# Attention in a decoder layer: ScalarE casts a turned tile ahead of the next tile's exponentials

## The chip, the core and the metric

One core of a Trainium2 chip runs the whole program. The metric is the time of one execution on the device in microseconds (us), as the median of several runs. The engines are PE (TensorE, matmuls and transposes), ACT (ScalarE), DVE (VectorE), POOL (GpSimd), and SP, whose queue issues most of the DMAs. Each engine works through its own instructions in a fixed order and waits for the others by semaphores.

## The reference

One layer (`DEPTH = 1`) of 1024 tokens with 1024 values each: forgetting attention with 16 heads of 64 values, a layer norm, then a mixture of 64 experts (8 per token) with one shared expert, and a second layer norm. The change touches attention alone:

```
for qb in range(S // Q):                       # Q = 128 queries
    t0, t1 = qb * Q, (qb + 1) * Q
    logits = einsum('bqhd,bkhd->bhqk', q[:, t0:t1], k[:, :t1]) * scale
    logits = logits + c[:, :, t0:t1, None] - c[:, :, None, :t1]
    p = softmax(where(causal, logits, -inf), axis=-1)
    outs.append(einsum('bhqk,bkhd->bqhd', p, v[:, :t1]))
```

`c` is a running sum of log gates. The softmax runs over the keys up to each query.

## The kernel before

Attention handles one head after another. Within a head it walks over eight query tiles of 128 queries, `t` = 0 to 7. Tile `t` has (t + 1) x 128 scores per query. They are cut into slots of at most 512 columns: tiles 0 to 3 have one slot each, tiles 4 to 7 have two, which makes 12 slots (0 to 11) a head. For every tile the work goes round three engines:

- PE computes the scores of a slot (lines 817 to 820) into one of three PSUM banks (`slot_banks`: two `bank`, one half of `out_ps`). The bank of slot n is free once the exponential of slot n - 3 has run.
- DVE takes the maximum of each slot (`maxima`, L1548) and, for two slots, the smaller of the two negated maxima (L1552). The result is `nm`.
- ACT takes the exponentials (`exponentials`, L1193) into `probs` (four buffers) and sums them.
- PE turns the slot, block by block, by transposes (`turns`, L847) into one of two banks of `k_ps` (`key_banks`).
- ACT casts the turned slot to its high half `pt_hi` (`turned_high`, L1204). DVE subtracts this to get the low half `pt_lo` (`turned_low`, L1559). The turned bank is free after that; turn number u waits for the low half of turn u - 2.
- PE multiplies high and low halves with the values (`weigh_v`, L868), once for tiles 0 to 3 of a head and once for tiles 4 to 7.

The order on each engine is written out by hand in a function `head` of its own. The turns lag by one tile: in step t PE computes the scores of tile t, some chunks of the next head's query and key projection (`project`, L80 to L82), and then turns the slots of tile t - 1. In step 0 the turned slots 10 and 11 are those of the head before, in step 2 PE also does `weigh_v` for the second half of the head before, and in step 5 for the first half of this head.

Other pieces sit between: `weights_hi`/`weights_lo` (L1165, L1500) split the next heads' projection weights; `take` moves a projected half from `q_ps` to SBUF (ACT L1184 and L1185, DVE L1539 and L1541); `low_values` (ACT L1212) and `normalise` (DVE L1574 and L1578) finish a half of a head's output. Turns 2 and 5 are not slots but the reciprocal sums (`rec`, L853). Turn 7 waits for `normalise` of the second half, as its bank holds those sums.

DVE's order within a step is: maxima of tile t, then `take` or `normalise` or weights where the step has them, then the low halves. In step 2 this reads: maximum of tile 2, `take` of the next head, low half of turn 4. In step 3: maximum of tile 3, `normalise`, low half of turn 6.

Of the kernel before, what the change touches and what calls it, by code (L numbers as in the profile page):

```python
# [5 lines left out]
P = 128  # L6
BANK = 512
ALU = mybir.AluOpType
# [4 lines left out]
AX_X = mybir.AxisListType.X  # L13
# [3 lines left out]
TT = T // P  # L17
# [67 lines left out]
def build(nc, x, w_in, b_f, w_out, ln1_g, ln1_b, router, router_bias, w_gate, w_up, w_down, ws_gate, ws_up,  # L85
          ws_down, ln2_g, ln2_b, out):
    with ExitStack() as ctx:
# [3 lines left out]
        def sb(n, s, d=F32, c=ctx):  # L91
            return c.enter_context(nc.sbuf_tensor(n, s, d))
# [27 lines left out]
        with ExitStack() as early:  # L120
# [3 lines left out]
            with ExitStack() as x1s:  # L124
                xt_hi = sb("xt_hi", [P, DC, T], F32R, c=x1s)
                xt_lo = sb("xt_lo", [P, DC, T], F32R, c=x1s)
                wqk = sb("wqk", [P, DC, P], c=x1s)
                wqk_hi = sb("wqk_hi", [P, DC, P], F32R, c=x1s)
                wqk_lo = sb("wqk_lo", [P, DC, P], F32R, c=x1s)
                with ExitStack() as a:  # L130
                    wv = sb("wv", [P, 2, DC, VC], c=a)
                    wv_hi = sb("wv_hi", [P, 2, DC, VC], F32R, c=a)
                    wv_lo = sb("wv_lo", [P, 2, DC, VC], F32R, c=a)
                    v_out = sb("v_out", [P, 2, 2 * VC // DH, 2, DH], F32R, c=a)
                    wf = sb("wf", [P, DC, HEADS], c=a)
                    wf_hi = sb("wf_hi", [P, DC, HEADS], F32R, c=a)
                    wf_lo = sb("wf_lo", [P, DC, HEADS], F32R, c=a)
                    bf = sb("bf", [P, HEADS], c=a)
                    zt = sb("zt", [HEADS, T], c=a)
                    z = sb("z", [P, TT, HEADS], c=a)  # L140
                    zabs = sb("zabs", [P, TT, HEADS], c=a)
                    zexp = sb("zexp", [P, TT, HEADS], c=a)
                    zlog = sb("zlog", [P, TT, HEADS], c=a)
                    zmin = sb("zmin", [P, TT, HEADS], c=a)
                    gate8 = sb("gate8", [P, TT, HEADS], c=a)
                    upto = sb("upto", [P, T], c=a)
                    c_hi = sb("c_hi", [HEADS, T], F32R, c=a)
                    c_lo = sb("c_lo", [HEADS, T], F32R, c=a)
                with ExitStack() as b:
                    qk = [[sb(f"{n}{i}", [P, T], F32R, c=b) for n in ("q_both", "q_ones", "k_twice", "k_rest")] for i in range(2)]  # L150
                    va = [sb(f"va{i}", [P, TT, P], F32R, c=b) for i in range(2)]
                    probs = [sb(f"probs{i}", [P, BANK], c=b) for i in range(4)]
                    pt_hi = sb("pt_hi", [P, TURNED, P], F32R, c=b)
                    pt_lo = sb("pt_lo", [P, TURNED, P], F32R, c=b)
                    heads_sum = sb("heads_sum", [DH, BANK], c=b)
                    nm = sb("nm", [P, TT], c=b)
                    nm2 = sb("nm2", [P, 2], c=b)
                    ssum = [sb(f"ssum{i}", [P, 2, TT], c=b) for i in range(2)]
                    rsum = sb("rsum", [P, TT // 2], c=b)
                    rec = [sb(f"rec{i}", [P, TT], c=b) for i in range(2)]  # L160
# [101 lines left out]
        S = {}  # L262
# [873 lines left out]
        def _(act):  # L1136
# [22 lines left out]
            def weights_hi(h, piece):  # L1159

                act.wait_ge(wqk_in[piece], 32 * h + 32)
                if not (static(h) and h == 0):
                    act.wait_ge(S["proj"], 3 * h + (piece - 1))
                c = slice(piece * DC // 2, (piece + 1) * DC // 2)
                a.copy(wqk_hi[:, c], wqk[:, c]).then_inc(S["wqk_hi_ok"], 1)  # L1165
# [15 lines left out]
            def take(h, par, half):  # L1181
                act.wait_ge(S["proj"], 3 * h + (2 * half + 1))
                r = slice(half * BANK, (half + 1) * BANK)
                a.mul(qk[par][0][0:DH, r], q_ps[0:DH, r], SCALE)  # L1184
                a.copy(qk[par][2][0:DH, r], q_ps[DH:P, r]).then_inc(S["ev_hi"], 1)  # L1185

            def exponentials(h, par, t):
                act.wait_ge(S["maxed"], TT * h + (t + 1))
                for k, n in enumerate(OF_TILE[t]):
                    w = SLOTS[n][2]  # L1190
                    if not (static(h) and NS * h + n < 4):
                        act.wait_ge(S["turned_ps"], NS * h + (n - 3))
                    a.activation(probs[n % 4][:, 0:w], slot_banks[n % 3][:, 0:w], ACT.Exp, bias=nm[:, t:t + 1],  # L1193
                                 accum_out=ssum[par][:, k, t:t + 1]).then_inc(S["exped"], 1)

            def turned_high(h, u):

                _, back, n = TURNS[u]
                act.wait_ge(S["turned_ps"], NS * h + (NS * back + n + 1))
                half = 0 if n < HALF_SLOTS[0] else 1  # L1200
                if not (static(h) and h + back < 1):
                    act.wait_ge(S["pv"], 2 * h + (2 * back + half - 1))
                b, step, count = turned_blocks(n)
                a.copy(pt_hi[:, b:b + (count - 1) * step + 1:step, :],  # L1204
                       key_banks[u % 2][:, 0:count * P].rearrange("p (j q) -> p j q", q=P)).then_inc(S["turned_hi"], 1)

            def low_values(h, half):

                act.wait_ge(S["pv"], 2 * h + (half + 1))
                if not (static(h) and 2 * h + half == 0):  # L1210
                    act.wait_ge(S["normed"], 2 * h + half)
                a.copy(heads_sum[:], pv_ps[DH:P, :]).then_inc(S["low_ok"], 1)  # L1212
# [6 lines left out]
            def head(p, par, first=False, left=HEADS):  # L1219
                h = 2 * p + par  # L1220
                for t in range(TT):
                    exponentials(h, par, t)
                    if t == 0 and not first:
                        if left > 1:
                            weights_hi(h + 1, 1)
                        turned_high(h, 0)
                        turned_high(h, 1)
                        take(h, par, 1)
                    elif t == 1:
                        turned_high(h, 3)  # L1230
                    elif t == 2:
                        if left > 1:
                            take(h + 1, 1 - par, 0)
                        turned_high(h, 4)
                    elif t == 3:
                        if not first:
                            low_values(h - 1, 1)
                        turned_high(h, 6)
                    elif t == 4:
                        turned_high(h, 7)  # L1240
                    elif t >= 5:
                        if t == 6 and left > 2:
                            weights_hi(h + 2, 0)
                        if t == 7:
                            low_values(h, 0)
                        for u in (2 * t - 2, 2 * t - 1):
                            turned_high(h, u)
                    if left == 1 and t >= 2:
                        split_wo(range(t - 2, t - 1))

# [233 lines left out]
        def _(dve):  # L1484
# [50 lines left out]
            def take(h, par, half):  # L1535
                q_both, _, k_twice, k_rest = qk[par]
                dve.wait_ge(S["ev_hi"], 2 * h + (half + 1))
                r = slice(half * BANK, (half + 1) * BANK)
                dve.scalar_tensor_tensor(out=q_both[DH:P, r], in0=q_ps[0:DH, r], scalar=SCALE, in1=q_both[0:DH, r], op0=ALU.mult,  # L1539
                                         op1=ALU.subtract)  # L1540
                dve.tensor_tensor(k_rest[0:DH, r], q_ps[DH:P, r], k_twice[0:DH, r], ALU.subtract).then_inc(S["ev_lo"], 1)  # L1541

            def maxima(h, t):

                for k, n in enumerate(OF_TILE[t]):
                    dve.wait_ge(S["score"], NS * h + (n + 1))
                    one = len(OF_TILE[t]) == 1
                    dve.tensor_reduce(nm[:, t:t + 1] if one else nm2[:, k:k + 1], slot_banks[n % 3][:, 0:SLOTS[n][2]], AX_X, ALU.max,  # L1548
                                      negate=True).then_inc(S["maxed"] if one else S["max_step"], 1)
                if not one:  # L1550
                    dve.wait_ge(S["max_step"], TT * h + 2 * (t - 3))
                    dve.tensor_tensor(nm[:, t:t + 1], nm2[:, 0:1], nm2[:, 1:2], ALU.min).then_inc(S["maxed"], 1)  # L1552

            def turned_low(h, u):
                _, back, n = TURNS[u]
# [432 lines left out]
```

## Time and profile before

| | us |
|---|---|
| median of 3 runs | 1902.46 |
| lowest and highest run | 1892.62, 1911.94 |
| the profiled execution, time | 1887.1 |
| its span in the trace | 1885.4 |
| PE busy | 1650.2 (88%) |
| DVE busy | 1200.7 (64%) |
| ACT busy | 1017.2 (54%) |
| stretch with attention, from the trace | about 155 to 690 of the span |
| one pair of heads within it | 64.8 to 64.9 |

The page's shares are means over the whole program. The experts (after 690 us) have other limits than attention. What an edit of attention is worth must be read inside the stretch of one head, where the timeline gives, for each engine, the start and length of each instruction and what ended the idle time before it.

### The profile page before, as it was taken

To read this page: it belongs to the slowest core of one execution; us is meant where nothing else is said; L and a number is where in the kernel's file an instruction comes from. 1 tells how busy PE (TensorE), PEld (TensorE's weight loads), DVE (VectorE), ACT (ScalarE), POOL (GpSimd) and SP (SyncE) were. 2 spreads that over 40 slices of the span, in tenths; PEclk is the share of its full clock that TensorE was granted. 3 is DMA by queue.
4 is the path that set the end of the run, shared out by engine and by line. 5 is a ranking of instruction groups with operands and counts; after the bars stand their busy time and mean duration, and the time that the engine had idled before them with its cause. 6 is when DMAs were issued, how large, how long until landed. Compare 5 with 4: busy or idle time off the path is not lost.

```text
span 1885.4 us, 31807 instructions
## 1 busy us (share of the span) xinstructions
PE 1650.2 (88%) x8302; PEld 1323.5 (70%) x8303; DVE 1200.7 (64%) x2030; ACT 1017.2 (54%) x1672; POOL 474.1 (25%) x486
## 2 busy tenths in 40 slices
PE   7995888888888859989999999999999999999960
PEld 5894666666676648777877777777777777787740
DVE  3212656556565556885566777777776777787836
ACT  3113545554555443333566676766766676777732
POOL 0000000000000000545144444444344443544420
PEclk9998999999999869889999999999999999999995
DMA  5313222212121214264799999998999899999956
GB/s 178 114 68 76 51 51 47 53 39 62 39 62 34 86 62 171 81 236 138 256 299 286 280 302 358 327 282 264 267 301 291 262 317 320 333 339 333 372 135 263
DMA packets 161508, 369.26 MB, mean 196 GB/s; under 512 B 53040, under 2 KB 73520, under 8 KB 161456
## 3 DMA queue, kind: packets, MB, share of 16 engines
q1 hardware_dynamic: 136272, 284.21, 44.2%
q0 software_dynamic: 25184, 84.39, 17.8%
q8 instruction: 28, 0.46, 0.1%
q14 instruction: 24, 0.20, 0.0%
HBM read 294.39 MB, written 65.77 MB: 191 GB/s over the span
## 4 chain that ended last, share of the span: by engine, by line
PE 46%; DVE 19%; issue 11%; DMA 11%; ACT 9%; POOL 2%; DVEq 1%; POOLq 1%; ACTq 1%; SPq 0%
DMA sums_scratch<-ys,sidx 5%; DVE nm L1548 5%; PE bank L969 4%; PE bank L975 4%; PE bank L972 4%; DVE pt_lo L1559 4%; PE out_ps L1027 3%; PE out_ps L1028 3%; DMA x_rows<-rows_scratch,gidx 3%; ACT probs L1193 3%; PE q_ps L959 3%; PE k_ps L1004 2%; PE k_ps L996 2%; PE k_ps L997 2%; PE bank L80 2%
## 5 line engine op out<-in xcount | busy, mean ns | idle before, releaser
L1778 DVE TENSOR_TENSOR gu_lo<-raw_gu,gu_hi 128x1024 fp32r<-128x1024 f32 x260 | 306.8, 1222 | 20.6 <-ACT gu_hi L1297 20.0
L1297 ACT CAST gu_hi<-raw_gu 128x1024 fp32r<-128x1024 f32 x260 | 252.7, 1048 | 0.0
L969 PE MATMUL bank<-gu_hi,xb_hi 128*128 128x512 f32 x576 | 235.0, 408 | 1.4 <-ACT ex L1289 1.3
L972 PE MATMUL bank<-gu_lo,xb_hi 128*128 128x512 f32 x576 | 227.6, 395 | 0.0
L1559 DVE TENSOR_TENSOR pt_lo<-k_ps,pt_hi 128x512 fp32r<-128x512 f32 (+1 forms) x192 | 100.9, 553 | 139.1 <-ACT pt_hi L1204 138.2
L1193 ACT ACTIVATE probs<-bank,nm 128x512 f32<-128x512 f32 (+3 forms) x128 | 73.9, 579 | 191.8 <-DVE nm L1552 107.6
L1778 DVE TENSOR_TENSOR dn_lo<-raw_dn,dn_hi 128x1024 fp32r<-128x1024 f32 x130 | 154.6, 1209 | 0.5 <-ACT dn_hi L1297 0.5
L641 POOL DMA_INDIRECT sums_scratch<-ys,sidx x64 | 114.2, 1784 | 131.4 <-DMA sums_scratch<-ys,sidx 76.8
L975 PE MATMUL bank<-gu_hi,xb_lo 128*128 128x512 f32 x576 | 146.2, 395 | 0.0
L576 POOL IOTA e<- 128x64 f32 x1 | 0.2, 190 | 550.6 <-DVE xs L1578 550.6
L1297 ACT CAST dn_hi<-raw_dn 128x1024 fp32r<-128x1024 f32 x130 | 129.5, 1046 | 0.0
L847 PE MATMUL k_ps<-ident,probs 128*128 128x128 f32 x576 | 94.5, 295 | 38.0 <-DVE pt_lo L1559 31.1
L969 PEld LDWEIGHTS bank<-gu_hi,xb_hi 128*128 128x128 f32 x576 | 109.5, 190 | 25.8 <-issue 2.5
L975 PEld LDWEIGHTS bank<-gu_hi,xb_lo 128*128 128x128 f32 x576 | 108.0, 187 | 26.4
L80 PE MATMUL q_ps<-xt_hi,wqk_hi 128*128 128x512 f32 x256 | 115.2, 450 | 11.9 <-DVE wqk_lo L1500 11.9
L972 PEld LDWEIGHTS bank<-gu_lo,xb_hi 128*128 128x128 f32 x576 | 108.9, 189 | 22.6
L996 PE MATMUL k_ps<-dn_hi,ht_hi 128*128 128x512 f32 x288 | 122.2, 424 | 1.4 <-ACT ht_hi L1326 1.4
L997 PE MATMUL k_ps<-dn_lo,ht_hi 128*128 128x512 f32 x288 | 117.6, 408 | 0.0
L847 PEld LDWEIGHTS k_ps<-ident,probs 128*128 128x128 f32 x576 | 70.9, 150 | 64.9 <-DVE pt_lo L1559 32.2
L959 PE MATMUL q_ps<-ident,x_rows 128*128 128x128 f32 x576 | 85.6, 295 | 29.8 <-DMA x_rows<-rows_scratch,gidx 24.1
L1318 ACT CAST xb_hi<-q_ps 128x1024 fp32r<-128x1024 f32 x72 | 73.1, 1016 | 67.3 <-PE q_ps L959 67.3
L1782 DVE TENSOR_TENSOR xb_lo<-q_ps,xb_hi 128x1024 fp32r<-128x1024 f32 x72 | 88.1, 1224 | 29.7 <-ACT xb_hi L1318 28.2
(268 smaller groups left out, 4123.8 us busy)
## 6 DMA issues: line engine op xcount, KB each, us to landing
raw_gu<-in_moe_w_gate_dram SPq DMA_DIRECT2D x128, 512.0 KB, 6.7
raw_gu<-in_moe_w_up_dram SPq DMA_DIRECT2D x128, 512.0 KB, 8.4
raw_dn<-in_moe_w_down_dram SPq DMA_DIRECT2D x128, 512.0 KB, 6.6
wqk<-in_fox_w_in_dram SPq DMA_DIRECT2D x66, 128.0 KB, 2.4
v_scratch<-v_out SPq DMA_DIRECT2D x32, 256.0 KB, 2.8
va<-v_scratch SPq DMA_DIRECT2D x16, 512.0 KB, 4.7
xs<-in_x_dram SPq DMA_DIRECT2D x8, 512.0 KB, 7.6
wv<-in_fox_w_in_dram SPq DMA_DIRECT2D x4, 1024.0 KB, 7.6
```

Of the source, the lines that this page charges most:

```text
L80: pe.matmul(out, w_hi, m_hi, start=start, stop=False, skip_group_check=True)
L847: i = pe.transpose(bank[:, j * P:(j + 1) * P], probs[n % 4][:, j * P:(j + 1) * P], ident[:])
L959: i = pe.transpose(ps[:, c * P:(c + 1) * P], v[:, c], ident[:])
L969: i = pe.matmul(o3, xb_hi[s][:, c], g_hi[:, :, c], start=c == 0, stop=False, skip_group_check=True)
L972: pe.matmul(o3, xb_hi[s][:, c], g_lo[:, :, c], start=False, stop=False, skip_group_check=True)
L975: i = pe.matmul(o3, xb_lo[s][:, c], g_hi[:, :, c], start=False, stop=c == DC - 1, skip_group_check=True)
L996: pe.matmul(k_ps[:, r], ht_hi[:, c], d_hi[:, c, r], start=c == 0, stop=False, skip_group_check=True)
L997: pe.matmul(k_ps[:, r], ht_hi[:, c], d_lo[:, c, r], start=False, stop=False, skip_group_check=True)
L1193: a.activation(probs[n % 4][:, 0:w], slot_banks[n % 3][:, 0:w], ACT.Exp, bias=nm[:, t:t + 1], accum_out=ssum[par][:, k, t:t + 1]).then_inc ...
L1297: a.copy(hi, raw).then_inc(S[done], 1)
L1559: dve.tensor_tensor(pt_lo[:, at, :], key_banks[u % 2][:, 0:count * P].rearrange("p (j q) -> p j q", q=P), pt_hi[:, at, :], ALU.subtract).t ...
L1778: dve.tensor_tensor(lo, raw, hi, ALU.subtract).then_inc(S[lo_ok], 1)
```

## The change

On ACT, each step of a head now begins with the casts of the slots that PE turns in that step, and the exponentials of the step's tile follow. Before, the exponentials came first and the casts were last in the step. The other pieces (`weights_hi`, `take`, `low_values` of the head before) keep their place behind the exponentials, and so now stand behind the casts too; `low_values` for the first half goes to the front of step 7. The two partial maxima of a tile get a place of their own for each tile (`nm2`). The orders of PE, DVE, POOL and SP stay as they were.

```diff
-                    nm2 = sb("nm2", [P, 2], c=b)
+                    nm2 = sb("nm2", [P, TT, 2], c=b)
...
                 for t in range(TT):
+                    if t == 7:
+                        low_values(h, 0)
+                    for u in ((0, 1), (3,), (4,), (6,), (7,), (8, 9), (10, 11), (12, 13))[t]:
+                        if not (first and TURNS[u][1]):
+                            turned_high(h, u)
                     exponentials(h, par, t)
                     if t == 0 and not first:
                         if left > 1:
                             weights_hi(h + 1, 1)
-                        turned_high(h, 0)
-                        turned_high(h, 1)
                         take(h, par, 1)
-                    elif t == 1:
-                        turned_high(h, 3)
-                    elif t == 2:
-                        if left > 1:
-                            take(h + 1, 1 - par, 0)
-                        turned_high(h, 4)
-                    elif t == 3:
-                        if not first:
-                            low_values(h - 1, 1)
-                        turned_high(h, 6)
-                    elif t == 4:
-                        turned_high(h, 7)
-                    elif t >= 5:
-                        if t == 6 and left > 2:
-                            weights_hi(h + 2, 0)
-                        if t == 7:
-                            low_values(h, 0)
-                        for u in (2 * t - 2, 2 * t - 1):
-                            turned_high(h, u)
+                    elif t == 2 and left > 1:
+                        take(h + 1, 1 - par, 0)
+                    elif t == 3 and not first:
+                        low_values(h - 1, 1)
+                    elif t == 6 and left > 2:
+                        weights_hi(h + 2, 0)
...
-                    dve.tensor_reduce(nm[:, t:t + 1] if one else nm2[:, k:k + 1], slot_banks[n % 3][:, 0:SLOTS[n][2]], AX_X, ALU.max,
+                    dve.tensor_reduce(nm[:, t:t + 1] if one else nm2[:, t, k:k + 1], slot_banks[n % 3][:, 0:SLOTS[n][2]], AX_X, ALU.max,
...
-                    dve.tensor_tensor(nm[:, t:t + 1], nm2[:, 0:1], nm2[:, 1:2], ALU.min).then_inc(S["maxed"], 1)
+                    dve.tensor_tensor(nm[:, t:t + 1], nm2[:, t, 0:1], nm2[:, t, 1:2], ALU.min).then_inc(S["maxed"], 1)
```

ACT's order in steps 2 to 4 of a middle head, before. L1193 is an exponential (128x384 is tile 2, the next 128x512 tile 3, then the two slots of tile 4), L1204 the cast of a turned slot (2x128 is turn 4, 3x128 turn 6, 4x128 turn 7), L1184 and L1185 the `take`, L1212 `low_values`:

```order
L1193 ACTIVATE probs,ssum<-out_ps,nm 128x384
L1184 ACTIVATE q_both<-q_ps 64x512
L1185 CAST k_twice<-q_ps 64x512
L1204 CAST pt_hi<-k_ps 128x2x128
L1193 ACTIVATE probs,ssum<-bank,nm 128x512
L1212 COPY heads_sum<-out_ps 64x512
L1204 CAST pt_hi<-k_ps 128x3x128
L1193 ACTIVATE probs,ssum<-bank,nm 128x512
L1193 ACTIVATE probs,ssum<-out_ps,nm 128x128
L1204 CAST pt_hi<-k_ps 128x4x128
```

And now, the same steps on ACT:

```order
L1204 CAST pt_hi<-k_ps 128x2x128
L1193 ACTIVATE probs,ssum<-out_ps,nm 128x384
L1184 ACTIVATE q_both<-q_ps 64x512
L1185 CAST k_twice<-q_ps 64x512
L1204 CAST pt_hi<-k_ps 128x3x128
L1193 ACTIVATE probs,ssum<-bank,nm 128x512
L1212 COPY heads_sum<-out_ps 64x512
L1204 CAST pt_hi<-k_ps 128x4x128
L1193 ACTIVATE probs,ssum<-bank,nm 128x512
L1193 ACTIVATE probs,ssum<-out_ps,nm 128x128
```

Each cast moved ahead of its step's exponential, of `take` in step 2 and of `low_values` in step 3.

ACT's order in steps 6 and 7 of a middle head, before. L1165 is `weights_hi`; the last two casts are turns 12 and 13, and the two 128x512 exponentials are slots 10 and 11:

```order
L1193 ACTIVATE probs,ssum<-out_ps,nm 128x512
L1193 ACTIVATE probs,ssum<-bank,nm 128x384
L1165 CAST wqk_hi<-wqk 128x512
L1204 CAST pt_hi<-k_ps 128x4x128
L1204 CAST pt_hi<-k_ps 128x2x128
L1193 ACTIVATE probs,ssum<-bank,nm 128x512
L1193 ACTIVATE probs,ssum<-out_ps,nm 128x512
L1212 COPY heads_sum<-out_ps 64x512
L1204 CAST pt_hi<-k_ps 128x4x128
L1204 CAST pt_hi<-k_ps 128x3x128
```

And now:

```order
L1204 CAST pt_hi<-k_ps 128x4x128
L1204 CAST pt_hi<-k_ps 128x2x128
L1193 ACTIVATE probs,ssum<-out_ps,nm 128x512
L1193 ACTIVATE probs,ssum<-bank,nm 128x384
L1165 CAST wqk_hi<-wqk 128x512
L1212 COPY heads_sum<-out_ps 64x512
L1204 CAST pt_hi<-k_ps 128x4x128
L1204 CAST pt_hi<-k_ps 128x3x128
L1193 ACTIVATE probs,ssum<-bank,nm 128x512
L1193 ACTIVATE probs,ssum<-out_ps,nm 128x512
```

Here two casts moved ahead of two exponentials, and `low_values` for the first half went with them.

## Rows read from the trace of the kernel before

**Rows 1.** The page's engines: busy us, share of the span, instructions.

```profile
PE 1650.2 (88%) x8302; PEld 1323.5 (70%) x8303; DVE 1200.7 (64%) x2030; ACT 1017.2 (54%) x1672; POOL 474.1 (25%) x486
```

**Rows 2.** PE in windows of two heads: length, busy, clock, DMA share, GB/s.

```profile
204.20:269.10 64.90, 56.05 (x298) 0.97 0.20 49
...
528.50:593.40 64.90, 56.17 (x298) 0.97 0.20 49
```

**Rows 3.** Who waited for whom, 204 to 630 us (12 to 13 heads): us, times, longest.

```profile
ACT probs L1193 <- DVE nm L1552: 114.0, 52, 2.7
DVE pt_lo L1559 <- ACT pt_hi L1204: 103.2, 52, 2.4
...
PE k_ps L847 <- DVE pt_lo L1559: 18.6, 24, 1.2
PE bank L817 <- ACT probs L1193: 14.6, 13, 1.2
PE q_ps L80 <- DVE wqk_lo L1500: 10.7, 13, 1.1
```

**Rows 4.** PE's timeline over one head: start, length, instruction, [idle before <- releaser].

```profile
412.67 0.50 PE L817 MATMUL out_ps<-k_twice,q_both 128*128 128x512 f32 x1 [0.66 <-ACT probs L1193]
...
414.95 0.99 PE L847 MATMUL k_ps<-ident,probs 128*128 128x128 f32 x7 [0.71 <-DVE pt_lo L1559]
416.34 0.32 PE L817 MATMUL bank<-k_twice,q_both 128*128 128x128 f32 x1 [0.40 <-issue]
...
417.32 0.50 PE L80 MATMUL q_ps<-xt_hi,wqk_hi 128*128 128x512 f32 x1 [0.48 <-DVE wqk_lo L1500]
...
420.17 1.09 PE L847 MATMUL k_ps<-ident,probs 128*128 128x128 f32 x8 [1.18 <-DVE pt_lo L1559]
...
421.80 0.28 PE L817 MATMUL bank<-k_twice,q_both 128*128 128x256 f32 x1
...
429.76 0.41 PE L847 MATMUL k_ps<-ident,probs 128*128 128x128 f32 x2
...
432.41 0.49 PE L847 MATMUL k_ps<-ident,probs 128*128 128x128 f32 x3
...
435.47 0.65 PE L847 MATMUL k_ps<-ident,probs 128*128 128x128 f32 x4 [0.42 <-DVE xs L1578]
...
437.79 0.39 PE L817 MATMUL bank<-k_twice,q_both 128*128 128x256 f32 x1 [1.19 <-ACT probs L1193]
```

**Rows 5.** ACT's timeline in steps 2 to 4 of the same head.

```profile
428.15 0.58 ACT L1193 ACTIVATE probs<-out_ps,nm 128x384 f32<-128x384 f32 x1 [1.43 <-DVE nm L1548]
...
430.20 0.37 ACT L1204 CAST pt_hi<-k_ps 128x256 fp32r<-128x256 f32 x1 [0.30 <-PE k_ps L847]
432.41 0.69 ACT L1193 ACTIVATE probs<-bank,nm 128x512 f32<-128x512 f32 x1 [1.84 <-DVE nm L1548]
...
433.21 0.58 ACT L1212 COPY heads_sum<-out_ps 64x512 f32<-64x512 f32 x1
433.82 0.48 ACT L1204 CAST pt_hi<-k_ps 128x384 fp32r<-128x384 f32 x1
```

**Rows 6.** DVE's timeline in the same steps.

```profile
429.93 0.68 DVE L1539 SCALAR_TENSOR_TENSOR q_both<-q_ps,q_both 64x512 fp32r<-64x512 f32 x1 [1.81 <-ACT k_twice L1185]
...
431.36 0.42 DVE L1559 TENSOR_TENSOR pt_lo<-k_ps,pt_hi 128x256 fp32r<-128x256 f32 x1
...
434.66 0.68 DVE L1578 TENSOR_TENSOR xs<-heads_sum,k_ps 64x512 f32 x1
435.37 0.56 DVE L1559 TENSOR_TENSOR pt_lo<-k_ps,pt_hi 128x384 fp32r<-128x384 f32 x1
435.85 0.68 DVE L1548 TENSOR_REDUCE nm<-bank 128x1 f32<-128x512 f32 x1
```

**Rows 7.** ACT's `low_values` in step 7 of three successive heads.

```profile
418.13 0.58 ACT L1212 COPY heads_sum<-out_ps 64x512 f32<-64x512 f32 x1
...
450.71 0.58 ACT L1212 COPY heads_sum<-out_ps 64x512 f32<-64x512 f32 x1
...
483.02 0.58 ACT L1212 COPY heads_sum<-out_ps 64x512 f32<-64x512 f32 x1
```

**Rows 8.** PE in two windows: length, busy, clock, DMA share, GB/s.

```profile
449.90:453.40 3.50, 3.31 (x9) 0.55 0.36 75
453.40:460.00 6.60, 6.60 (x38) 0.98 0.28 61
```

## The prediction

> **What bounds the kernel now.** I read the page's engines first: PE is busy 88% of the span, DVE 64%, ACT 54% [rows 1]. Attention alone, in windows of two heads, gives 64.9 us a pair with PE busy 56.1 of them; six windows in a row, of which the first and last are shown, differ by 0.1 us [rows 2]. So a head takes 32.4 us, PE works 28 of them (with its drains counted as work), and an edit to the order of ACT can win at most what PE waits. The waits [rows 3] show a circle. ACT's exponentials wait 114.0 us for the maxima, DVE's low halves wait 103.2 us for ACT's casts: in a step, DVE's maxima, ACT's exponentials, ACT's casts and DVE's low halves run one behind the other, although casts and low halves belong to the tile before and need nothing of this step's maxima. PE sees the end of that circle at three places a head: transposes behind a low half, 24 times and 18.6 us, scores behind an exponential, and the projection behind `wqk_lo`. The timeline of one head [rows 4] gives their size: idle 0.71, 0.40, 0.48 and 1.18 us from step 7 of a head to step 0 of the next, 0.42 before turn 7, and 1.19 and 0.66 before the second slot of tiles 5 and 7.
>
> **Part 1, what the new order wins: steps 7 and 0.** The casts of turns 12, 13, 0 and 1 no longer wait for the exponentials, so the low halves, the maxima behind them and `weights_lo` all run earlier. From the second slot's scores of tile 7 (412.67) to the scores of tile 1 (421.80) PE takes 9.13 us [rows 4]. The work in it, at the spacing at which unhindered matmuls of that head start (0.235 us for 512 columns, which is three to a projection chunk of 0.70; about 0.1 us a transpose), is 0.55 for the scores, four chunks 2.8, 15 transposes 1.5, tile 0's scores 0.3: 5.15 us. I leave 0.25 for a shorter wait on `wqk_lo`, whose DVE instruction still stands behind the maxima of tile 7. Gain: 9.13 - 5.4 = 3.7 us. The four idle pieces alone are 2.77, so the gain lies between 2.8 and 4.0.
>
> **Part 2, what it loses in step 0.** `weights_hi` for the second piece stands behind the two casts, and these behind PE's turns 0 and 1. After these turns: cast about 0.5, exponential 0.37, `weights_hi` 0.6, `weights_lo` 0.7, and four hand-overs of about 0.1: 2.6 us. PE has a chunk, tile 1's scores and another chunk to do, 1.7 us. Loss 0.9 us (before, the projection did not wait there at all); between 0.5 and 1.2.
>
> **Part 3, what it loses in steps 2 to 4.** In step 2 PE does 3.1 us of `weigh_v` before turn 4. The exponential of tile 2 and `take` ran under that (428.15 [rows 5]); now they stand behind the cast of turn 4 and cannot start before about 430.2. DVE's FIFO carries the delay on: its `take` is ahead of the low half of turn 4, for which turn 6 waits. From the cast at 430.20: cast 0.37, exponential 0.58, ACT's `take` until DVE begins 1.2, DVE's `take` 1.43 (429.93 to 431.36), low half 0.42 [rows 5, 6]; turn 6 starts at 434.25 in place of 432.41 [rows 4]. In step 3 the same again: turn 6 0.49, cast 0.48, exponential 0.80, `low_values` 0.62, DVE's sum 0.83 and product until PE starts 0.81; turn 7 starts at 438.3 in place of 435.47. In step 4 DVE's low half of turn 6 (0.48) and the two maxima (435.85 until ACT starts, 1.10) follow the product, then the exponential 0.84: the second slot of tile 5 comes at 440.7 in place of 437.79. Loss 2.9 us. The nearest bound from below is half of that, if DVE and ACT overlap more than I have them; from above 3.3. I take 2.8, as the hand-overs are counted twice in places.
>
> **Part 4, steps 5 to 7.** A second slot's scores (tiles 6 and 7) need the exponential of the first slot of the tile before, and this stands now behind two casts that wait for PE's own turns. For tile 7: last turn until the cast is done about 0.5, exponential 0.7, against the first slot's scores 0.5 that PE has meanwhile. The wait stays near 0.7 to 1.1 us, as it was (0.66). Turn 9 and `weigh_v` no longer wait for a low half, 0.2 us. Net 0.2 gained, between 0.5 gained and 0.5 lost. The two instructions for `nm2` only write to other addresses: nothing. The DMAs and SP's and POOL's queues keep their order; their waits (`copied`, `wqk_in`) are issued several us before they are needed, and I cost them at nothing.
>
> **Sum without the clock.** -3.7 + 0.9 + 2.8 - 0.2 = -0.2 us a head. The first head has no head before it, the last no projection; I count 15 heads: -3 us.
>
> **Part 5, the clock.** In the pairs of [rows 2] the mean granted clock is 0.97. It falls once a pair: from 449.9 on PE ran 9 matmuls in 3.5 us at a clock of 0.55 (the lower level, 1.2 GHz, for most of it), behind the idle pieces between steps 7 and 0; then it is back [rows 8]. There it costs little, since PE had another 1.18 us of idle behind it to eat into: the head with it took 32.58 us, the next 32.31 [rows 7]. The change moves the holes. They now stand before turn 6 (1.8), turn 7 (1.3) and the second slot of tile 5 (1.3), within some 7 us, and behind the last of them PE has 6 us of work with hardly a wait. A stretch of 3.4 us at half rate costs 1.7 there less what little slack there is, 1.4 us, if it falls there. How often is not to be had from these rows. Bounds: never (0) and in every head (1.7 us a head). I take two heads in five, near the one in two of now, since the new holes are larger but those between steps 7 and 0 close: 1.4 x 0.4 = 0.56 us a head. What the clock costs now, 32.58 - 32.31 = 0.27 a pair or 0.14 a head [rows 7], goes off: 0.4 us a head, 6 us in all. The Trainium skill (TensorE: Matmul & The Clock Gate, "What's actually happening") says that the ramp's penalty is under 1% of a typical span and not to be fitted; by that the clock's term would be left out and the time would be 1899. The rows' 1% is the very bound that decides here, so I keep it.
>
> **The number.** -3 + 6 = +3 us. The profiled execution took 1887.1 us, so its like would take 1890; it stood 15 us (0.8%) below the median, all of which I put to the spread of runs (1892.62 to 1911.94). Against the median: 1902.5 + 3 = 1905.5, rounded to 1906.
>
> **The rivals.** "Within 1%" (19 us) is about what a measurement of this kernel can tell from no change.
>
> A, the forecast: gains in steps 7 and 0 and losses in steps 2 to 4 cancel; 1906, its own range 1893 to 1918. For it: the two chains are read from the same head, row by row. Chance 0.64.
>
> B, slower: the clock drops in every head. The place is the stretch behind the second slot of tile 5; the price 1.7 us x 15 = 25 us, with part 1 to 4's -3 and the present clock loss given back (-2): 1923. It decides if the idle before turns 6 and 7 and that slot (4.4 us of 8) lowers the clock each time. For it: now the clock falls behind idle pieces that together are 2.8 us of 8, but only in every second head; so the point is near. Against: the pair of holes varies by head. The Trainium skill has this as a rule (same page, "HAM oscillation — how this bites in real kernels"): a loop that waits too long in each turn starts each turn at the lower clock. By that rule it is this rival's time. With losses at their upper bounds B reaches 1930. Chance 0.19.
>
> C, faster: DVE and ACT take up the delay of step 2, as in part 3's lower bound or better. Only the gains of parts 1 and 4 and part 2's loss stay: (-3.7 + 0.9 - 0.2) x 15 = -45 us, 1857; with half of part 3, -3 + 6 - 21 = -18 us, 1884. It decides if `take` did not have to wait for the cast; against it stands the written order, which leaves ACT nothing else to do. Chance 0.10.
>
> D, the order does not matter: the casts in their new place end no earlier because PE's turns are late anyway. ACT's cast at 430.20 waited for PE by 0.30 [rows 5], which speaks for it in step 2; the 103.2 us speak against it elsewhere. 1902. Chance 0.07.
>
> **Range and chances.** The range takes A's and most of B's, and the near end of C: 1887 to 1926. Slower by over 1% (above 1921.5): most of B and a little of A, 0.17. Faster by over 1% (below 1883.4): C, 0.10. Same: 0.73.
>
> **What would show it.** In the profile after: PE's idle before the transposes and the first projection chunk between steps 7 and 0 gone or under 0.3 us (part 1); a wait for `wqk_lo` of about 0.9 between tile 1's first and second projection chunk (part 2); transposes x3 idle 1.8 behind `pt_lo` and transposes x4 idle over 1 behind `xs` (part 3); DVE's low halves waiting far less than 103.2 us, ACT's casts waiting for PE tens of us instead; a pair of heads of 64.5 to 66 us; low clock after the scores of tile 5 and not between heads (part 5). The prediction is wrong if the waits in steps 2 and 3 are under half of what I have, or if a pair takes over 67 us.

## The result: 1.2% slower

| | before | changed |
|---|---|---|
| median of 11 runs, us | 1894.56 | 1920.06 |
| lowest to highest | 1886.65 to 1911.94 | 1912.74 to 1922.92 |
| profiled execution, time / span | 1887.1 / 1885.4 | 1913.6 / 1911.9 |

The ratio to before is 1.0116, with a 95% interval of 1.0088 to 1.0144. That is also the ratio of the means of the 11 runs, 1918.4 and 1896.4 us, so the change costs 22 us; the two medians alone would give 1.0135.

The first thing to see in the profile after is what did not change. The page's engine line (busy us, share of the span, instructions), to be read against [rows 1], has the same instruction counts, and busy times within 1%:

```profile
PE 1657.4 (87%) x8302; PEld 1331.0 (70%) x8303; DVE 1204.1 (63%) x2030; ACT 1016.5 (53%) x1672; POOL 472.5 (25%) x486
```

So no work was added; the 26.5 us of span are waiting and clock. PE in windows of two heads (length, busy, clock, DMA share, GB/s), against 64.9 us and a clock of 0.97 in every pair before [rows 2]:

```profile
223.90:289.70 65.80, 54.69 (x300) 1.00 0.21 49
289.70:358.60 68.90, 57.78 (x299) 0.95 0.19 46
358.60:428.70 70.10, 58.99 (x299) 0.93 0.19 45
428.70:497.10 68.40, 57.30 (x298) 0.95 0.19 46
497.10:562.80 65.70, 54.60 (x298) 1.00 0.20 48
```

Two pairs are at full clock, and take 65.7 to 65.8 us: this is the price of the new waits alone, 0.4 us a head. The other three hold the lower clock in part and take 2.7 to 4.4 us more. The mean of the five is 67.8 us, over the 67 at which the prediction calls itself wrong. The waits of PE in 204 to 630 us (us in total, times, longest), the answer to [rows 3]:

```profile
PE k_ps L847 <- DVE pt_lo L1549: 21.4, 13, 1.7
PE k_ps L847 <- DVE xs L1568: 16.9, 13, 1.3
PE bank L817 <- ACT probs L1193: 14.8, 13, 1.2
PE out_ps L817 <- ACT probs L1193: 12.3, 13, 0.9
PE q_ps L80 <- DVE wqk_lo L1490: 6.1, 12, 0.5
```

Transposes waited 24 times for a low half before, twice a head and up to 1.2 us; now once a head and 1.7 us. The wait for `xs` (the product of `normalise`) is new in this size; before, it was 2.7 us in 6 waits. The waits behind ACT and DVE turned over:

```profile
ACT pt_hi L1204 <- PE k_ps L847: 213.5, 100, 3.8
DVE q_both L1529 <- ACT k_twice L1185: 54.4, 13, 4.4
DVE pt_lo L1549 <- ACT pt_hi L1204: 47.6, 38, 2.2
DVE wqk_lo L1490 <- ACT wqk_hi L1165: 31.7, 12, 2.6
```

DVE's low halves wait 47.6 us for ACT's casts where it was 103.2, as the change wanted. But ACT now stands 213.5 us at the casts for PE's turns, and DVE 54.4 us at its `take`, behind ACT's. (L1529, L1531, L1538, L1549 and L1568 are the lines that were L1539, L1541, L1548, L1559 and L1578 before.)

**One head on PE after**, start, length, instruction, [idle before <- releaser], the answer to [rows 4], at full clock:

```profile
426.75 0.50 PE L817 MATMUL out_ps<-k_twice,q_both 128*128 128x512 f32 x1 [0.95 <-ACT probs L1193]
428.15 0.93 PE L847 MATMUL k_ps<-ident,probs 128*128 128x128 f32 x7
...
430.68 1.19 PE L847 MATMUL k_ps<-ident,probs 128*128 128x128 f32 x8
432.41 0.28 PE L817 MATMUL bank<-k_twice,q_both 128*128 128x256 f32 x1
434.15 0.50 PE L80 MATMUL q_ps<-xt_hi,wqk_hi 128*128 128x512 f32 x1 [0.51 <-DVE wqk_lo L1490]
...
441.26 0.40 PE L847 MATMUL k_ps<-ident,probs 128*128 128x128 f32 x2
...
445.73 0.55 PE L847 MATMUL k_ps<-ident,probs 128*128 128x128 f32 x3 [1.65 <-DVE pt_lo L1549]
...
449.75 0.66 PE L847 MATMUL k_ps<-ident,probs 128*128 128x128 f32 x4 [1.32 <-DVE xs L1568]
...
452.07 0.39 PE L817 MATMUL bank<-k_twice,q_both 128*128 128x256 f32 x1 [1.20 <-ACT probs L1193]
```

From the second slot of tile 7 to tile 1's scores it is 5.66 us (9.13 before); from turn 4 to the second slot of tile 5 it is 10.81 us (8.03 before). Steps 2 and 3 on ACT, the answer to [rows 5]:

```profile
441.70 0.37 ACT L1204 CAST pt_hi<-k_ps 128x256 fp32r<-128x256 f32 x1 [3.56 <-PE k_ps L847]
441.97 0.59 ACT L1193 ACTIVATE probs<-out_ps,nm 128x384 f32<-128x384 f32 x1
...
442.54 0.58 ACT L1184 ACTIVATE q_both<-q_ps 64x512 fp32r<-64x512 f32 x1
443.13 0.58 ACT L1185 CAST k_twice<-q_ps 64x512 fp32r<-64x512 f32 x1
446.31 0.48 ACT L1204 CAST pt_hi<-k_ps 128x384 fp32r<-128x384 f32 x1 [2.59 <-PE k_ps L847]
```

ACT stands idle for 3.56 us at the cast, and the exponential and `take` run only then. DVE's maximum of this tile was ready from 439.70 on (the first line below), so for the last 2.0 us of that idle time the exponential could have run. DVE's `take` follows at 443.75 after 4.05 us of idle, the answer to [rows 6]:

```profile
439.15 0.55 DVE L1538 TENSOR_REDUCE nm<-out_ps 128x1 f32<-128x384 f32 x1
443.75 0.68 DVE L1529 SCALAR_TENSOR_TENSOR q_both<-q_ps,q_both 64x512 fp32r<-64x512 f32 x1 [4.05 <-ACT k_twice L1185]
444.45 0.69 DVE L1531 TENSOR_TENSOR k_rest<-q_ps,k_twice 64x512 fp32r<-64x512 f32 x1
445.17 0.42 DVE L1549 TENSOR_TENSOR pt_lo<-k_ps,pt_hi 128x256 fp32r<-128x256 f32 x1
```

**The lower clock** moved as well. Before, it fell once in two heads, between heads [rows 8]. Two windows of PE after, the answer to them:

```profile
415.70:422.50 6.80, 6.28 (x21) 0.51 0.00 0
422.50:428.00 5.50, 4.55 (x24) 0.99 0.00 0
```

The first begins in PE's idle time before the second slot of tile 5 (416.22 us), behind the holes before turns 6 and 7 (a hole is idle time of PE), and covers `weigh_v` and the scores of tile 6. The head with it took 35.8 us, the next one 32.85.

### The profile page after: what moved, and what is told of

It is laid out like the page before. It is cut to its first block, busy times and chain, and to the rows that moved or that the text cites. A ratio compares the mean times of both kernels' runs of the same rounds, so it can differ in the third digit from the quotient of the medians.

```text
span 1911.9 us, 31807 instructions
## 1 busy us (share of the span) xinstructions
PE 1657.4 (87%) x8302; PEld 1331.0 (70%) x8303; DVE 1204.1 (63%) x2030; ACT 1016.5 (53%) x1672; POOL 472.5 (25%) x486
## 4 chain that ended last, share of the span: by engine, by line
PE 60%; DVE 11%; issue 10%; DMA 9%; ACT 5%; POOL 2%; POOLq 1%; DVEq 1%; another core or an unknown queue 1%; ACTq 0%; SPq 0%
DMA sums_scratch<-ys,sidx 4%; PE bank L969 4%; PE bank L972 4%; PE out_ps L868 4%; PE bank L975 4%; PE q_ps L80 4%; PE out_ps L1027 3%; PE k_ps L847 3%; DMA x_rows<-rows_scratch,gidx 3%; PE out_ps L1028 3%; PE q_ps L82 3%; PE q_ps L81 3%; PE q_ps L959 3%; PE k_ps L1004 2%; PE k_ps L996 2%
## 5 line engine op out<-in xcount | busy, mean ns | idle before, releaser
L1204 ACT CAST pt_hi<-k_ps 128x512 fp32r<-128x512 f32 (+1 forms) x192 | 86.4, 481 | 261.7 <-PE k_ps L847 261.4
L641 POOL DMA_INDIRECT sums_scratch<-ys,sidx x64 | 110.3, 1724 | 131.2 <-DMA sums_scratch<-ys,sidx 73.2
L1549 DVE TENSOR_TENSOR pt_lo<-k_ps,pt_hi 128x512 fp32r<-128x512 f32 (+1 forms) x192 | 100.8, 553 | 66.2 <-ACT pt_hi L1204 65.3
L847 PEld LDWEIGHTS k_ps<-ident,probs 128*128 128x128 f32 x576 | 72.2, 151 | 74.7 <-issue 47.6
```

The source lines that it names most:

```text
L641: g.indirect_dma_start(out=sums[0], out_offset=bass.IndirectOffsetOnAxis(ap=sidx[par][:, 0:1], axis=0), in_=ys[par][:], in_offset=None, co ...
L847: i = pe.transpose(bank[:, j * P:(j + 1) * P], probs[n % 4][:, j * P:(j + 1) * P], ident[:])
L1549: dve.tensor_tensor(pt_lo[:, at, :], key_banks[u % 2][:, 0:count * P].rearrange("p (j q) -> p j q", q=P), pt_hi[:, at, :], ALU.subtract).t ...
```

## The experiments

All ratios are to the kernel before, run on the same chip. The stages of a head, from PE's timeline, as means over 10 to 12 middle heads in us; the fifth stage is that of the heads at full clock:

| stage of a head | before | e1 | changed | e2 | e5 | e6 |
|---|---|---|---|---|---|---|
| scores tile 1 to turn 4 (steps 1, 2) | 7.93 | 7.93 | 8.89 | 7.92 | 8.89 | 8.89 |
| turn 4 to turn 6 | 2.65 | 2.66 | 4.47 | 2.65 | 2.65 | 2.66 |
| turn 6 to turn 7 | 2.80 | 3.01 | 4.02 | 2.59 | 3.02 | 3.97 |
| turn 7 to second slot of tile 5 | 2.25 | 2.25 | 2.25 | 2.25 | 2.25 | 2.25 |
| to second slot of tile 7, full clock | 7.47 | 7.47 | 7.55 | 7.55 | 7.53 | 7.54 |
| to tile 1's scores of the next head | 9.35 | 9.13 | 5.66 | 5.66 | 5.66 | 5.65 |
| sum | 32.45 | 32.45 | 32.84 | 28.62 | 30.00 | 30.96 |

**e1, the wider `nm2` alone.** Edit against the kernel before:

```diff
-                    nm2 = sb("nm2", [P, 2], c=b)
+                    nm2 = sb("nm2", [P, TT, 2], c=b)
```

> ACT's order as before; only the wider place for the two partial maxima is kept. Every theory that puts the 25 us to the order of casts and exponentials expects the time of the kernel before: ratio 1.000, within 0.3%, and 32.3 and 32.6 us for heads in turn. If the wider tile itself cost something (another address on DVE), this kernel would be slower by part of the 1.2%.

Measured 1885.69 us, ratio 0.9996 (0.9970 to 1.0022). The wider tile costs nothing that can be measured, so the difference is the order's.

This trace shows one thing more. Here too the clock fell once in two heads, between heads. PE at one fall, and in a pair of heads with one:

```profile
415.70:419.00 3.30, 3.13 (x13) 0.50 0.00 0
325.20:390.10 64.90, 56.13 (x298) 0.97 0.21 49
```

But the stage with the fall took 9.13 us, the same stage without it 9.12 to 9.13: the waits behind the fall shrank by what the transposes took longer. In the trace of before, the fall came later in that stage and cost 0.4 us there (9.56 in place of 9.13), which the next head got back before turn 7 (2.5 against 2.9 in e1). So the two stages of before that differ from e1 are mixed with the clock, and their sum is not: the order's own gain between heads is 9.13 - 5.66 = 3.47 us, its loss before turn 7 is 4.02 - 3.01 = 1.01 us, and the falls before the change cost nothing in sum.

**e2, the cast ahead in steps 4 to 7 alone.** Edit against the changed kernel:

```diff
                 for t in range(TT):
...
+                    ahead = t in (4, 5, 6, 7)
...
+                    if ahead:
+                        if t == 7:
+                            low_values(h, 0)
+                        for u in us:
                             turned_high(h, u)
                     exponentials(h, par, t)
...
+                    if not ahead and (t > 0):
+                        if t == 7:
+                            low_values(h, 0)
+                        for u in us:
+                            turned_high(h, u)
```

`us` are the turns of the step. In step 0, if it is not ahead, the casts stand between `weights_hi` and `take`, as before.

> Only in steps 4 to 7 of a head does the cast go ahead of the exponentials; steps 0 to 3 are as before. Theory (gain and loss in different steps): the gain between steps 7 and 0 stays (3.7 us a head), the wait for wqk_lo in step 0 and the chain through steps 2 and 3 are gone, so 28 to 29 us a head in place of 32.4, some 3.5 to 4.3 us x 14.5 = 50 to 62 us less: ratio 0.967 to 0.975. Rival (the circle of DVE and ACT is only moved, PE waits the same in sum wherever the casts stand): within 1% of before, 32 us a head.

Measured 1828.02 us, ratio 0.9693 (0.9662 to 0.9725): 3.1% faster. PE in pairs of heads:

```profile
216.80:274.10 57.30, 53.10 (x300) 1.00 0.23 56
274.10:331.30 57.20, 53.03 (x298) 1.00 0.23 55
```

28.6 us a head, and the clock did not fall in any middle head. The rival is out: PE's waits are not conserved. The stage between heads takes the same 5.66 us as in the changed kernel, so its gain comes from steps 4 to 7 alone; what the move of `low_values` in step 7 has in it was not tested by itself. Two heads in turn:

```profile
334.90:363.70 28.80, 26.66 (x150) 1.00 0.23 55
363.70:392.10 28.40, 26.38 (x149) 1.00 0.23 56
```

They differ by 0.3 us at full clock, as those before the change did with its fall (32.58 and 32.31 [rows 7]). That difference is one of even and odd heads, not the price of the clock.

**e3, the cast ahead in steps 0 to 3 alone** (the same edit with `(0, 1, 2, 3)`).

> The complement: the cast goes ahead in steps 0 to 3 alone. Theory: the losses of steps 0, 2 and 3 without the gain, 3.5 to 4 us a head more than before, plus more drops of PE's clock: 36 to 37.5 us a head, 52 to 75 us more, ratio 1.028 to 1.040. Rival (the slowdown of the change is the clock's alone, its waits cancel inside steps 0 to 3 too): not over 1.015.

Measured 1958.57 us, ratio 1.0384 (1.0351 to 1.0418), as expected. Heads 1 to 5 take 36.0 to 36.9 us; heads 6 to 13 take 37.5 to 37.7, with a drop of the clock in each. That rules out the rival: the waits of these steps do not cancel.

**e4, the changed kernel with PE kept busy in its holes.** Edit:

```diff
+            def keep_busy(bank, count):
+                for _ in range(count):
+                    pe.matmul(bank[:, 0:BANK], xt_hi[:, 0, 0:P], xt_hi[:, 0, 0:BANK], start=True, stop=True, skip_group_check=True)
...
+                    if n == 7 and not (static(h) and h in (0, HEADS - 1)):
+                        pe.wait_ge(S["turned_lo"], NS * h + 3)
+                        keep_busy(key_banks[0], 3)
...
+                        if not (static(h) and h in (0, HEADS - 1)):
+                            pe.wait_ge(S["exped"], NS * h + 2)
+                            keep_busy(slot_banks[1], 6)
+                        turns(h, par, (6,), first)
...
+                        if not (static(h) and h in (0, HEADS - 1)):
+                            pe.wait_ge(S["exped"], NS * h + 4)
+                            keep_busy(slot_banks[0], 4)
                         turns(h, par, (7,), first)
```

> The changed kernel, with 6, 4 and 3 extra matmuls of 512 columns (results overwritten) that PE runs in its three waits of steps 3 to 5 (before turn 6, before turn 7, before the second slot of tile 5) in heads 1 to 14. They add 13 x 0.235 = 3.1 us of work a head inside 4.0 us of waiting. Theory (16 of the 25 us are the lower clock behind these waits): the drops of the clock in steps 4 and 5 vanish, each head takes 32.9 to 33.1 us in place of 34.1, and the time falls by 13 to 17 us against the change: ratio to before 1.002 to 1.005. Rival (the loss is in the waits themselves, and the lower clock is hidden in them): no gain, ratio 1.012 or more, as the extra matmuls only delay what follows.

Measured 1886.57 us, ratio 0.9997 (0.9977 to 1.0017): more matmuls, and 1.2% less time than the change. PE in pairs of heads:

```profile
225.10:290.80 65.70, 60.68 (x325) 1.00 0.21 49
290.80:356.50 65.70, 60.65 (x325) 1.00 0.20 48
356.50:422.10 65.60, 60.54 (x324) 1.00 0.20 48
```

The clock did not fall in heads 1 to 14, and each head takes 32.8 us, the changed kernel's length at full clock. Where the changed kernel took 32.8 to 35.8, the extra work of 3 us a head came for nothing. This shows the clock's part by itself. By the ratios the gain is above the 13 to 17 us expected. In the traces attention gave 15.1 us (its last `normalise` product starts at 704.7 in place of 719.8); the rest came from behind it, on which more below.

**e5, ahead in all steps but 2 and 3; e6, in all but 2** (the same edit with those steps).

> The cast goes ahead in all steps but 2 and 3. Against e2 (steps 4 to 7: 28.6 us a head, ratio 0.969) this adds the casts ahead in steps 0 and 1. Theory: weights_hi behind the casts of turns 0 and 1 makes PE wait for wqk_lo in step 0 by 0.5 to 0.9 us, and a head takes 29.5 to 30 us: ratio 0.976 to 0.980. Rival (the low halves of step 0 come earlier and pay for it): 28.6 us, ratio 0.969.

> The cast goes ahead in all steps but 2. Theory (part 3: the delay has a first piece in step 2, where take stands behind the cast that waits for weigh_v, and a second in step 3, where low_values stands behind the cast): with the first piece gone and the second left, 30.2 to 30.9 us a head, ratio 0.982 to 0.989. Rival (step 3 loses nothing by itself): as e5. Other rival (the pieces do not add up, the one only covers the other): near the change, over 1.00.

Measured: e5 1856.05 us, 0.9829 (0.9788 to 0.9869); e6 1867.36 us, 0.9907 (0.9875 to 0.9938). In the table, e5 against e2 adds 0.97 us up to turn 4 and 0.43 before turn 7, 1.4 a head where 0.9 to 1.4 was expected. e6 against e5 adds 0.95, all before turn 7. The change against e6 adds 1.8 before turn 6. So the pieces add up, in the places where the chain puts them. Both ratios came out above what was expected (0.976 to 0.980, and 0.982 to 0.989). The clock explains about as much: it fell in 4 of heads 1 to 14 in e5 and in 3 of them in e6, for 1.6 us each, 6.4 and 4.8 us or 0.003.

**e7, e2 with step 6 split**: the exponential of the first slot ahead of the two casts, that of the second behind them.

```diff
-            def exponentials(h, par, t):
+            def exponentials(h, par, t, slots):
...
+                    if t == 6:
+                        exponentials(h, par, t, OF_TILE[t][:1])
                     if ahead:
...
                         for u in us:
                             turned_high(h, u)
-                    exponentials(h, par, t)
+                    exponentials(h, par, t, OF_TILE[t][1:] if t == 6 else OF_TILE[t])
```

> As e2, and in step 6 the exponential of the first slot goes ahead of the two casts, that of the second slot behind them. Theory: the second slot's scores of tile 7 wait 0.94 us a head for that exponential, which stands behind casts that wait for PE's own turns; it becomes free earlier, and a head takes 27.9 to 28.2 us in place of 28.6: ratio 0.961 to 0.966. Rival (the low halves then wait for the exponential and PE waits for them instead): 28.6 us, 0.969.

Measured 1814.27 us, ratio 0.9619 (0.9578 to 0.9659): the best version, 3.8% faster than before. The stage from the second slot of tile 5 to that of tile 7 went from 7.55 to 6.43 us; 0.66 us was lost again between heads (6.32 against 5.66); the later second exponential is the likely reason, not tested by itself. A head takes 27.9 us, and the clock did not fall in heads 1 to 14.

**e8, the changed kernel again.**

> The changed kernel once more, for a second trace. In the first one attention took 16 to 17 us more than before and the stages behind it 9 to 10 us more (routing 6, first experts 4), where nothing was changed. Theory: both come from when the lower clock falls there, so the second trace shows another amount behind attention, anything from 0 to 10 us; the ratio stays 1.009 to 1.014. Rival: something in the change costs these 10 us each time (then the same stages show the same 6 and 4 us again).

Measured 1907.48 us, ratio 1.0114 (1.0065 to 1.0164). Attention ended 19.2 us later than in the trace of before, and the stages behind it took the same time as there, within 1 us (span 1904.1). So the extra 9.8 us behind attention in the first trace are not the change's each time. The clock fell in 8 of heads 1 to 14, four times for 6.8 us; in the first trace it was 9 heads, three times for 6.8. PE over routing and the first experts, before, changed, changed again:

```profile
700.00:922.00 222.00, 204.73 (x1007) 0.92 0.46 161
```

```profile
716.50:949.00 232.50, 209.78 (x1011) 0.90 0.44 154
```

```profile
719.50:943.00 223.50, 207.05 (x1009) 0.92 0.46 161
```

The longest of the three has the lowest clock. From the end of attention's last product to the end of the program the traces took 1181.6 (before), 1176.7 (e1), 1191.4 (changed), 1181.1 (changed again) and 1176.7 us (e4). That the clock's falls make these differences fits the rows above, but was not shown by itself.

## Why the prediction was right and wrong

The range held the time; the forecast within it did not come. It said 3 us more than before and no change that can be told; measured are 22 us more, 1.2%. The chance for slower by over 1% had been put at 0.17. That the time lies in the range is partly luck: the range stood on the median of three runs, 1902.46 us, and that of the eleven is 8 us lower. Laid around that one it would have been 1879 to 1918, and 1920 would have missed it. By its own sign, a pair of over 67 us, the prediction was wrong. Point by point, per head:

- **Part 1, the gain in steps 7 and 0**: 3.7 us predicted, 3.47 measured (9.13 in the head that was read, and in e1, to 5.66). Right in its place, 0.2 too large: PE waits for nothing there any more, and its work alone takes 5.66 us, where 5.15 had been counted, and 0.25 for a wait. e2 keeps the gain without steps 0 to 3.
- **Part 2, the loss in step 0**: 0.9 predicted, 0.96 measured up to turn 4 (8.89 - 7.93), with the named wait for `wqk_lo` (0.51 us idle in the timeline). Right in place and size.
- **Part 3, steps 2 to 4**: 2.8 taken, worked out as 2.9, measured 2.78 in heads of the kind that was read (10.81 - 8.03), and 2.82 in the means (1.81 + 1.01). The places are the ones named: idle 1.65 before turn 6 and 1.32 before turn 7. Whether hand-overs were counted twice, as the correction from 2.9 to 2.8 says, no run shows.
- **Part 4**: 0.2 gained predicted, 0.08 lost measured (7.47 to 7.55). The wait for the exponential before tile 7's second slot grew from 0.66 to 0.95 and ate the cast's gain. This and part 1 turn the sum without the clock from -0.2 into +0.39 (32.84 - 32.45): 0.6 us a head, 8 us in the whole.
- **Part 5, the clock**: this is the step that failed, by its size. Its mechanism, place and price were right: it falls behind the holes before turns 6 and 7 and in that of slot 7, onto PE's dense work, and a fall of 3.4 us costs 1.6 us (9.15 against 7.55; 1.4 to 1.7 said). The frequency was not: two heads in five, against 9 of heads 1 to 14 in the first trace, and in three of them the lower clock lasted 6.8 us and cost 2.8 to 3.0. All in all 18 us, 1.29 us a head in place of 0.56 (17.5 us, 1.25 a head, in e8's trace). I had taken a number near that of before though the holes were the larger; the length of a fall I took from the only kind that I had read in the trace of before. The 0.14 a head that part 5 took off for what the clock cost before was wrong too: e1 and e2 show that the 0.27 us behind it is the difference of even and odd heads. e4 confirms the term: take the falls away and the time falls by 1.2%.
- From tile 1's scores of head 1 to those of head 15 the sum is 14 x (0.39 + 1.29) = 23.5 us; 24.0 us was measured there. In front of that stretch the change saves 3.2 us and behind it, in the last head, 4.1, on which the prediction had put nothing; so attention as a whole ended 16.7 us later.

Rival B came nearest. Its time, 20.5 us above the base, fits the 22 measured, though by another sum: the clock fell not in every head but in 9 of 14, some of the falls were twice as long, and 5.5 us are the waits', which it had at -3.

Of the other rivals, C (DVE and ACT take up step 2's delay) is ruled out by ACT's 3.56 us of idle at the cast; what it said would happen "if `take` did not have to wait" did happen in e6, where it does not: 0.9907, where its 1884 of 1902 is 0.990. D is ruled out by the shorter waits of DVE's low halves (47.6 us from 103.2) and the 3.47 us between heads.

The Trainium skill (TensorE: Matmul & The Clock Gate, "What's actually happening") puts the penalty of the ramp under 1% of a typical span and says not to fit a count of slow matmuls. Here the measured clock term is 15 us by e4 and 18 us by the stages, of 1895: 0.8 to 1.0%, no more than the page says, but as large as the whole question. The same page ("HAM oscillation — how this bites in real kernels") tells of a loop in which one long wait for a DMA in each turn lowers the clock for the next. The trace agrees in that the clock fell in 9 of 14 heads, and in e3 in all from the sixth on. It differs in the waits: those of PE were many and short, none in heads 1 to 14 over 1.7 us, and the clock fell behind three of them close together.

## What to carry to other kernels

In a queue that works in a fixed order, put the instruction first whose input comes first in that step. The same swap of cast and exponential gained 3.5 us a head between heads (steps 4 to 7) and lost 2.8 in steps 2 and 3; e6 puts 1.8 of these to step 2, where PE has 3 us of other matmuls to do before the turn that the cast waits for. Judge such a swap step by step, with what stands behind each of the two on every other engine, and apply it only where it pays (e2, e7). When a reordering joins PE's waits into one region ahead of its densest work, count the lower clock as a cost of its own; e4 shows how to test it, by giving PE throw-away matmuls in the holes. Before you read a price off two heads in turn, check in a trace at full clock that they don't differ anyway.

## What was not expected of the hardware

- Adding work made the kernel faster: 13 more matmuls of 512 columns a head (3.1 us of PE) took the time from 1.0116 to 0.9997 of before, since the granted clock stayed at its upper level.
- The same 3.4 us of lower clock cost 1.6 us where PE had dense work (the change) and nothing where it had waits behind it to shorten (e1).
- In heads 1 to 14 the lower clock came in lengths of 3.4 and of 6.8 us. One of the longer ones ran 21 matmuls at a clock of 0.51 in 6.8 us with PE busy for 6.28 of them; why it did not rise after the first 3.4 us is open.
- Hardly anything else of a middle head varies: at full clock each stage repeats within 0.1 us among the heads of one parity (every second head), and in the two traces of the changed kernel. A chain worked out from one head held to 0.3 us a part.
